# A hybrid recurrent decoder: the decode tails of three branches move into the streamed work, each behind a later gate, and two branches' ways up move further back

## Chip, cores and metric

The program runs on one core of one Trainium2 chip. The metric is the device time of one execution in microseconds; a kernel is timed several times, and its median is what counts. One execution is also profiled, and every row of the trace comes from that one.

## What is computed

Two layers of a decoder on 256 prompt tokens and 8 decode tokens (264 columns in all; the decode tokens bring states of their own). Each layer is a mixer and then a feed-forward network: a dense SwiGLU in the first layer, the best two of eight experts in the second. The mixer, cut to its frame:

```
u = x @ w_in + b_in                     # projections of four branches, and gates
o_a, S1 = _rwkv7(rw, ...)               # RWKV-7: decay, delta rule, per-token scan
o_b, C1, n1, m1 = _mlstm(mqk, mv, ...)  # mLSTM: matrix memory, then head norm
o_c, gS1 = _gla(gq, gk, gv, gg, ...)    # GLA: decaying state, then head rms
o_d, h1 = _rglru(rx, ry, ...)           # RG-LRU: gated linear recurrence
branches = jnp.stack([o_a, o_b, o_c, o_d], axis=2)
up = jnp.einsum('blgc,gcd->blgd', branches, p['w_branch'][l])
gate = jax.nn.sigmoid(gates.reshape(B, L, N_BRANCH, D))
out = jnp.einsum('blgd,blgd->bld', gate, up) @ p['w_out'][l]
```

The prompt part of a branch is done in chunks. The eight decode tokens each take one step from their state, for GLA for instance

```
S = decay * S + k v^T ;  y = q S        # per decode token; S is an output too
```

In this text the **tail** of a branch is this decode step and, for mLSTM and GLA, the norm over heads and the multiplication by the branch's gate that follow it, since the norm runs over all 264 columns at once.

## The kernel before

**Engines.** PE (TensorE) multiplies, DVE (VectorE) and ACT (ScalarE) do the arithmetic between, SP (SyncE) loads weights through a ring of slots, POOL loads states and parameters. Each has its instructions in a fixed order and waits on semaphores that others raise; the names of the steps ("rw.ops", "n1.var") are those of the semaphore groups.

**Branch work.** In each layer the branches come in the order RG-LRU, mLSTM, GLA, RWKV. Their matmuls write `mW`, four banks of PSUM. The work is a chain that changes engines at nearly every step.

**Streamed work.** Beside it stands work that has no tight order. `streamed_work` (L52) lists it: 13 pairs of projections, 16 pairs of gates (four for each branch), and after each gate the way up of the branch one gate earlier (`("up", g, q)`), except RWKV's four, which end the list. A projection or gate pair needs, on ACT, rounding of its weights in two halves (L824) and reading of its two result tiles (L830, L837); on DVE, the difference between weight and rounded weight, in two halves (L1270, "low parts" or "splits"); on PE, 48 matmuls of 264 columns, two thirds with the rounded weight (`XH`, `XL` are the rounded activations and their rest). A way up is four matmuls on PE (fp32), two products with the gate on DVE (L1279) and a sum (L1285). Their results go through `mA`, the other four banks of PSUM, in the order of the list: tile n takes bank n mod 4 and waits until tile n - 4 has been read.

**The order.** Each engine runs the list through its own generator. `filler` (L687) takes a table (`PE_FILL`, `ACT_FILL`, `DVE_FILL`), and `fill("rw.ops")` issues as many streamed items as the table has for that name, ahead of the wait of that name. So the tables decide, engine by engine, how much streamed work lies between two steps of the chain. On DVE `link` (L1214) makes the next instruction wait until the one before has been written.

**Tails.** They are part of the chain. mLSTM's tail begins behind the step ml.cout: a product with the identity spread over 512 columns (`mm(mW, bo, MX)`, ml.dvb), DVE's update of the state, a second such product (ml.dnum), then `head_norm` (L1292 on DVE, L1992 on PE, L845 on ACT): mean, square, variance, root, reciprocal. GLA's (gl.dvb, gl.dy, n2) begins behind gl.y, RWKV's (rw.dsa, rw.dy) behind rw.bonus and ahead of rw.ops, L1593 to L1607 on DVE.

```
PE_FILL:  "rw.g": 19, "rw.dx": 70, "rw.dr": 51, "rw.ops": 49, "rw.again0": 15
DVE_FILL: "rw.bonus": 1, "loads12": 1, "rw.exp": 1, "rw.dsa": 3, "rw.dy": 3, "rw.turn": 4
```

Behind the mixer come a layer norm, the SwiGLU or the experts. They are not touched.

## Time and profile before

| | us |
|---|---|
| runs (three) | 1965.49, 1957.01, 1965.77; median 1965.49 |
| the profiled execution's own time | 1960.32 |
| its span in the profile | 1958.5 |
| PE, DVE, ACT busy in the span | 1805.5, 1383.6, 939.5 |
| mean granted clock of PE | 0.954 |

The span runs from the first to the last instruction of the profiled execution; its own time has 1.8 us more around it. The mixer of layer 0 takes the first 400 us of the span, that of layer 1 from about 620 to 1014 us, the experts the rest. A row of the timeline gives start, duration and instruction, with the idle time of that engine ahead of it and what ended that in square brackets. A granted clock of 1.00 is 2.4 GHz, one of 0.50 is 1.2 GHz; a mean between them is a mix of the two.

### The profile page before, as it was taken

How to read it: one execution, taken by the hardware profiler on the slowest of the kernel's cores; microseconds unless marked ns; L12 is line 12 of the kernel's file. 1: busy time of each engine (PE TensorE's matmuls, PEld its weight loads, DVE VectorE, ACT ScalarE, POOL GpSimd, SP SyncE). 2: the span in 40 equal slices, each digit the busy share in tenths (PEclk: the TensorE clock that was granted, in tenths of full speed). 3: DMA queues.
4: the chain of work that ended last, by engine and by line, in shares of the span. 5: the costliest groups of instructions: out<-in, count | busy, mean ns of one | idle time of the engine just before them, and what ended most of it. 6: DMA issues, size and time to landing. Idle time of an engine off the chain costs nothing.

```text
span 1958.5 us, 26391 instructions
## 1 busy us (share of the span) xinstructions
PE 1805.5 (92%) x10174; PEld 1527.9 (78%) x10174; DVE 1383.6 (71%) x1619; ACT 939.5 (48%) x968; POOL 15.2 (1%) x32
## 2 busy tenths in 40 slices
PE   8799989979998989989986999999899999999896
PEld 7678878879997868868865877777687877777685
DVE  4857864445652758885425988989797979888794
ACT  4323422243332524422214666666576657766673
POOL 1000000000001000000000000000000000000000
PEclk9789999999998979999995999999999999999999
DMA  6233322334552324321223988989798978989770
GB/s 244 94 107 141 123 87 72 124 151 173 186 182 77 130 87 159 127 97 65 109 105 155 343 320 298 346 305 340 272 347 306 340 282 323 346 320 344 278 299 23
DMA packets 59307, 402.81 MB, mean 206 GB/s; under 512 B 8672, under 2 KB 9344, under 8 KB 11312
## 3 DMA queue, kind: packets, MB, share of 16 engines
q1 hardware_dynamic: 54144, 393.73, 54.0%
q0 software_dynamic: 1600, 3.97, 0.6%
q10 hardware_dynamic: 3440, 3.41, 0.5%
q8 instruction: 84, 1.38, 0.3%
q14 instruction: 39, 0.32, 0.0%
HBM read 396.60 MB, written 4.49 MB: 205 GB/s over the span
## 4 chain that ended last, share of the span: by engine, by line
PE 81%; DVE 11%; ACT 4%; issue 3%; DMA 0%; ACTq 0%; DVEq 0%; SPq 0%
PE mA L1906 48%; PE mW L1906 31%; ACT WH L703 2%; DVE slots_rounded L1270 1%; PE mA L1837 1%; DVE SCR L1235 1%; ACT X L994 1%; DVE SCR L1352 0%; DMA slots<-in_w_in_dram 0%; DVE V L1709 0%; DVE SCR L1347 0%; PE mW L1909 0%; DVE BIG L1285 0%; DVE HEL L1172 0%; DVE SCR L1237 0%
## 5 line engine op out<-in xcount | busy, mean ns | idle before, releaser
L1050 DVE TENSOR_TENSOR ring_low<-ring,WH 128x2048 fp32r<-128x2048 f32 x216 | 493.0, 2289 | 92.6 <-ACT WH L703 92.0
L703 ACT ACTIVATE WH<-ring 128x2048 fp32r<-128x2048 f32 x212 | 405.0, 1913 | 79.6 <-PE mW L1906 64.4
L1906 PE MATMUL mA<-XH,slots_rounded 128*128 128x264 f32 x1696 | 378.3, 297 | 10.2 <-DVE slots_rounded L1270 9.2
L1906 PE MATMUL mA<-WH,XEH 128*128 128x512 f32 x704 | 293.9, 418 | 8.2 <-DVE XEL L1140 6.9
L1906 PEld LDWEIGHTS mA<-XH,slots_rounded 128*128 128x128 f32 x1696 | 286.5, 194 | 17.8 <-issue 12.7
L1906 PE MATMUL mA<-WH,XEL 128*128 128x512 f32 x704 | 277.0, 393 | 0.0
L1906 PE MATMUL mA<-ring_low,XEH 128*128 128x512 f32 x608 | 240.2, 395 | 0.0
L1906 PE MATMUL mA<-XL,slots_rounded 128*128 128x264 f32 x672 | 197.2, 293 | 6.5 <-DVE small L1549 5.6
L1906 PEld LDWEIGHTS mA<-WH,XEH 128*128 128x128 f32 x704 | 133.1, 189 | 39.3 <-DVE ring_low L1050 10.6
L1906 PEld LDWEIGHTS mA<-WH,XEL 128*128 128x128 f32 x704 | 132.9, 189 | 31.9
L1906 PEld LDWEIGHTS mA<-XL,slots_rounded 128*128 128x128 f32 x672 | 130.3, 194 | 11.4 <-DVE small L1549 7.3
L1906 PE MATMUL mA<-BIG,slots 128*128 128x264 f32 x512 | 126.3, 398 | 10.8 <-DVE SCR L1630 6.7
L837 ACT ACTIVATE BIG<-mA,half 128x264 f32<-128x264 f32 x64 | 30.5, 480 | 220.1 <-PE mA L1906 220.1
L1906 PE MATMUL mW<-WH,HEH 128*128 128x512 f32 x352 | 114.7, 408 | 19.1 <-DVE HEL L1172 19.1
L1906 PEld LDWEIGHTS mA<-ring_low,XEH 128*128 128x128 f32 x608 | 114.8, 189 | 22.1
L1050 DVE TENSOR_TENSOR more_low<-more_ring,WH 128x2048 fp32r<-128x2048 f32 x48 | 109.9, 2289 | 17.8 <-ACT WH L703 17.6
L1906 PEld LDWEIGHTS mA<-BIG,slots 128*128 128x128 f32 x512 | 97.8, 196 | 29.9 <-DVE SCR L1630 7.2
L1270 DVE TENSOR_TENSOR slots_rounded<-slots,slots_rounded 128x1024 fp32r<-128x1024 f32 x84 | 100.9, 1223 | 17.4 <-ACT slots_rounded L824 15.7
L1906 PE MATMUL mW<-WH,HEL 128*128 128x512 f32 x352 | 112.8, 402 | 0.0
L1012 ACT ACTIVATE FWH<-slots 128x2048 fp32r<-128x2048 f32 x34 | 65.3, 1920 | 76.0 <-PE mA L1906 46.7
L703 ACT ACTIVATE WH<-more_ring 128x2048 fp32r<-128x2048 f32 x48 | 91.9, 1915 | 20.1 <-PE mW L1906 16.6
L755 ACT ACTIVATE HEH<-mA 128x256 fp32r<-128x256 f32 x88 | 33.7, 383 | 137.7 <-PE mA L1837 137.6
(396 smaller groups left out, 3135.7 us busy)
## 6 DMA issues: line engine op xcount, KB each, us to landing
ring<-in_moe_dram SPq DMA_DIRECT2D x216, 1024.0 KB, 4.8
slots<-in_w_in_dram SPq DMA_DIRECT2D x58, 1024.0 KB, 4.8
more_ring<-in_moe_dram SPq DMA_DIRECT2D x48, 1024.0 KB, 4.8
...
```

Source lines behind the costliest of these rows:

```text
L703: nact.activation(WH[:, HI_SLOT[j % PAIR], :], expert_slot(j), ACT.Copy).then_inc(weights_hi, 1)
L755: nact.activation(HEH[:, b, :], mA[:, 2 + b, 0:256], ACT.Copy).then_inc(turned_hi, 1)
L837: nact.activation(GT[:, gate % GR, :], acc("gate", l, gate), ACT.Tanh, scale=0.5, bias=hc("bgate", KT * item[1] + 2 * item[2] + q))\
L994: ins = nact.activation(X[:, j, :], SQ8[:, j, :], ACT.Identity, scale=pc(f"ln{i + 1}g", j), bias=pc(f"ln{i + 1}b", j))
L1012: nact.activation(w.rounded, w.raw, ACT.Copy).then_inc(hi_done, 2)
L1050: v.tensor_tensor(expert_low(j), expert_slot(j), WH[:, HI_SLOT[j % PAIR], :].bitcast(F32), SUB)\
L1235: v.scalar_tensor_tensor(dst[:, i, back:TP], src[:, i, 0:TP - back], pc(w, 4 * i + 3 - back), dst[:, i, back:TP], MUL, ADD)
L1270: v.tensor_tensor(halves_of(w.low, half), halves_of(w.raw, half), halves_of(w.rounded, half).bitcast(F32), SUB).then_inc(lo_done, 1)
L1837: ins = nc.tensor.transpose(mA[:, 2 + b, P * q:P * q + P], HT[:, b, P * q:P * q + P], C("ident"))
L1906: return nc.tensor.matmul(out, w, x, start=start, stop=stop, skip_group_check=True)
```

## The change

Nine pieces of the tails become streamed items of their own. Each stands in the list directly behind a gate (the third of RG-LRU to the third of GLA), and their 22 matmuls write banks of `mA` in turn with the gates' tiles. On DVE, the steps of a tail are items in the stream too, between the two halves of the splits that follow that gate; on ACT the square and the root of the norms, and the stores of the states, come a gate later. The ways up follow their gates at a distance: RG-LRU one gate behind, mLSTM three, GLA two, RWKV at the end. All three tables of fills are new; DVE's may now name any `link` of the chain ("link23": 1). States are loaded earlier by POOL with a semaphore each, stores of decode states count on a semaphore of their own, the scratch tiles lie elsewhere, and three small copies keep operands of the tails alive.

```diff
+TAILS = {(RG, 2): "ml.dvb", (RG, 3): "ml.dnum", (ML, 0): "ml.mean", (ML, 1): "ml.var", (ML, 2): "gl.dvb", (ML, 3): "gl.dy", (GL, 0): "gl.var", (GL, 1): "rw.dsa", (GL, 2): "rw.dy"}
+
+BEHIND = {RG: 1, ML: 3, GL: 2, RW: 4}
 def streamed_work():
     seq = [("u", i) for i in (TMI - 1, TRX, TRY, TMQ, TMK, TMV, TMO, TGQ, TGV, TGG, TR, TK, TV)]
-    late = []
-    for g in (RG, ML, GL, RW):
-        for q in range(4):
-            seq.append(("gate", g, q))
-            late.append(("up", g, q))
-            if len(late) > 1 and late[0][1] != RW:
-                seq.append(late.pop(0))
-    return seq + late
+    gates = [(g, q) for g in (RG, ML, GL, RW) for q in range(4)]
+    ups = list(gates)
+    for n, (g, q) in enumerate(gates):
+        seq.append(("gate", g, q))
+        while ups[0][0] != RW and gates.index(ups[0]) + BEHIND[ups[0][0]] <= n:
+            seq.append(("up",) + ups.pop(0))
+        if (g, q) in TAILS:
+            seq.append(("tail", TAILS[g, q]))
+    return seq + [("up",) + up for up in ups]
...
-PE_FILL = {"loads9": 25, "rg.conv": 95, "ml.qk": 228, "ml.logd0": 16, "ml.kw3": 9, "ml.abs": 7, "ml.h": 44,
+PE_FILL = {"loads9": 25, "rg.conv": 112, "rg1": 473, "ml.gcol": 15, "ml.kw3": 10, "ml.abs": 8, "ml.h": 34,
...
             def link(ins):
                 linked[0] += 1
+                links[0] += 1
+                own = linked[0]
                 ins.then_inc(dve_link, 1)
-                dve.wait_ge(dve_link, linked[0])
+                between[0](f"link{links[0]}")
+                dve.wait_ge(dve_link, own)
...
+                if name == "gl":
+                    dve.wait_ge(decoded_out, 16 * (DECODED * l + 3))
+                    dve.wait_ge(*act_of.at("u.tile", l, 17))
+                    yield from named(v.tensor_tensor(GXX, unit(), over_v(U[:, TGV:TGV + 2, TP:T]), MUL), "gt.dv")
+                    dve.wait_ge(gl_state_in, 16 * (l + 1))
+                    dve.wait_ge(*act_of.at("gl.exp", l))
+                    yield from linked_up(v.tensor_tensor(GS, GS, over_gv(GDX), MUL))
+                if name == "gl.dvb":
+                    dve.wait_ge(*pe_of.at("gt.dvb", l))
...
             def streamed():
-                l, up, n = layer[0], 0, 0
+                l, up, n, behind = layer[0], 0, 0, []
                 for item in STREAM:
+                    if item[0] == "tail":
+                        behind.append(item[1])
+                        continue
                     if item[0] != "up":
                         n += 1
-                        if PLAIN <= n < len(PAIRS):
+                        for name in behind:
+                            yield from tail_of(name)
+                        if n < len(PAIRS) and n >= PLAIN:
...
+                        while behind:
+                            yield from tail_of(behind.pop(0) + " rest")
+                        if TAILS.get(item[1:]) in ("ml.dvb", "gl.dvb", "rw.dsa"):
+                            yield from tail_of(TAILS[item[1:]][0:2])
...
+                    if name == "gl.dvb":
+                        pe.wait_ge(*dve_of.at("gt.dv", l))
+                        out = into(0)
+                        for j in range(2):
+                            ins = mm(out, con[:, CC["gv"] + P * j:CC["gv"] + P * j + P], flat(GXX, j), j == 0, j == 1)
+                            if j:
+                                ins.then_inc(*pe_of.step("gt.dvb"))
+                            yield
...
-                fill("rw.dx")
-                pe.wait_ge(*dve_of.at("rw.dx", l))
-                for j in range(2):
-                    mm(mW[:, j, :], bo, DX[:, j, :, :].rearrange("p b v -> p (b v)"))
-                for j in range(2):
-                    ins = mm(mW[:, 2 + j, :], bo, DY[:, j, :, :].rearrange("p b v -> p (b v)"))
-                ins.then_inc(*pe_of.step("rw.dsa"))
```

What this does to the order is shown at three places. The first is DVE in RG-LRU, from the step behind the decay's exponential (TENSOR_SCALAR 128x530) through the six steps of a series; `slots_rounded` as the result is a low part, `SCR` scratch of the branch. Before:

```order
L1346 TENSOR_SCALAR SCR<-SCR 128x530 [waits lg_act]
L1347 RECIPROCAL SCR<-SCR 128x530 [waits dve_link]
L1348 TENSOR_TENSOR SCR<-SCR 128x530 [waits dve_link]
L1349 TENSOR_TENSOR SCR<-SCR 128x530 [waits dve_link]
L1350 TENSOR_SCALAR SCR<-SCR 128x530 [waits dve_link]
L1352 SCALAR_TENSOR_TENSOR SCR<-SCR 128x530 [waits dve_link] x6
L1353 TENSOR_SCALAR SCR<-SCR 128x530 [waits dve_link]
```

and now:

```order
L1531 RECIPROCAL SCR<-SCR 128x530 [waits dve_link]
L1453 TENSOR_TENSOR slots_rounded<-slots,slots_rounded 128x1024 [waits hi_done]
L1532 TENSOR_TENSOR SCR<-SCR 128x530 [waits dve_link]
L1453 TENSOR_TENSOR slots_rounded<-slots,slots_rounded 128x1024 [waits hi_done]
L1533 TENSOR_TENSOR SCR<-SCR 128x530 [waits dve_link]
L1453 TENSOR_TENSOR slots_rounded<-slots,slots_rounded 128x1024 [waits hi_done]
L1534 TENSOR_SCALAR SCR<-SCR 128x530 [waits dve_link]
L1453 TENSOR_TENSOR slots_rounded<-slots,mg_rounded 128x1024 [waits hi_done]
L1536 SCALAR_TENSOR_TENSOR SCR<-SCR 128x530 [waits dve_link]
L1453 TENSOR_TENSOR slots_rounded<-slots,mg_rounded 128x1024 [waits hi_done]
L1536 SCALAR_TENSOR_TENSOR SCR<-SCR 128x530 [waits dve_link] x3
```

Low parts now stand between the linked steps, each with a wait for ACT's rounding of its half (hi_done); up to the mLSTM's q and k there are 14 halves more than before.

The second place is PE in RWKV. `mW<-SCR,con 128x264` is the bonus product, `128x512` a tail's product, `mA<-XH` and `mA<-XL` streamed matmuls. Before, RWKV's tail stands there, behind 70 streamed items:

```order
L1906 MATMUL mW<-SCR,con 128x264 [waits rw_dve,rw_act]
L1906 MATMUL mW<-SCR,con 128x264
...
L1906 MATMUL mA<-BIG,slots 128x264 [waits mg.up_dve]
L1906 MATMUL mA<-BIG,slots 128x264
L1906 MATMUL mW<-SCR,con 128x512 [waits rw_dve]
L1906 MATMUL mW<-SCR,con 128x512 x3
L1906 MATMUL mA<-XH,slots_rounded 128x264 [waits lo_done,gate.tile_act]
```

Now:

```order
L2021 MATMUL mW<-SCR,con 128x264 [waits rw_dve,rw_act]
L2021 MATMUL mW<-SCR,con 128x264
L2021 MATMUL mA<-XH,slots_rounded 128x264
L2021 MATMUL mA<-SQ_62,con 128x264 [waits n1_dve,n1_act]
L2021 MATMUL mA<-SQ_62,con 128x264 [waits n1_dve]
L2021 MATMUL mA<-XH,slots_rounded 128x264 [waits lo_done,gate.tile_act]
...
L2021 MATMUL mA<-SCR,con 128x512 [waits n1_dve,gt_dve]
L2021 MATMUL mA<-SCR,con 128x512
L2021 MATMUL mA<-XH,slots_rounded 128x264 [waits lo_done,gate.tile_act]
```

RWKV's tail is gone from here. The variance of mLSTM's norm (`SQ_62`) and, 48 streamed matmuls later, the first product of GLA's tail have come in its place, the latter with a wait for DVE (gt_dve).

The third place is DVE in the same stretch, from the reciprocal of RWKV's key norm (128x528) on. Before:

```order
L1577 RECIPROCAL SCR<-SCR 128x528 [waits rw_act]
L1579 SCALAR_TENSOR_TENSOR SCR<-BIG,par,SCR 128x264 [waits dve_link]
L1579 SCALAR_TENSOR_TENSOR SCR<-BIG,par,SCR 128x264
L1279 SCALAR_TENSOR_TENSOR V_59<-BIG,mA 128x264 [waits gate.tile_act,mg.up_pe,dve_link]
L1583 TENSOR_TENSOR BIG<-mW,BIG 128x528 [waits rw_pe]
L1585 SCALAR_TENSOR_TENSOR SCR<-con,SCR 128x256 [waits rw_dve]
L1585 SCALAR_TENSOR_TENSOR SCR<-con,SCR 128x256
L1587 TENSOR_TENSOR SCR<-SCR 128x512 [waits dve_link]
L1589 TENSOR_TENSOR SCR<-SCR 128x16 [waits rw_dve]
L1590 TENSOR_TENSOR SCR<-con,BIG 128x1024
```

and now, from the same reciprocal to gt.dv, the row that PE's product above waits for:

```order
L1706 RECIPROCAL SCR<-SCR 128x528 [waits rw_act]
L1453 TENSOR_TENSOR slots_rounded<-slots,slots_rounded 128x1024 [waits hi_done,n1_dve]
L1453 TENSOR_TENSOR slots_rounded<-slots,slots_rounded 128x1024 [waits hi_done]
...
L1383 RECIPROCAL SQ_62<-SQ_62 128x528 [waits n1_act]
L1712 TENSOR_TENSOR BIG<-mW,BIG 128x528 [waits rw_pe,dve_link]
L1714 SCALAR_TENSOR_TENSOR SCR<-con,SCR 128x256 [waits rw_dve]
...
L1384 TENSOR_TENSOR V_59<-V_59,SQ_62 128x528 [waits tail_link]
L1716 TENSOR_TENSOR SCR<-SCR 128x512 [waits dve_link]
...
L1391 SCALAR_TENSOR_TENSOR BIG<-V_59,par,BIG 128x264 [waits tail_link]
L1393 SCALAR_TENSOR_TENSOR BIG<-V_59,par,BIG 128x264
L1399 TENSOR_TENSOR SCR<-con,BIG 128x1024 [waits u.tile_act,decoded_out,mt_dve]
```

The end of mLSTM's tail (`SQ_62`, `V_59`), with a reciprocal of its own, now lies between RWKV's steps and ahead of gt.dv.

## Rows read from the trace of the kernel before

**Rows 1.** The page: busy time by engine; the chain by engine.

```profile
PE 1805.5 (92%) x10174; PEld 1527.9 (78%) x10174; DVE 1383.6 (71%) x1619; ACT 939.5 (48%) x968; POOL 15.2 (1%) x32
...
PE 81%; DVE 11%; ACT 4%; issue 3%; DMA 0%; ACTq 0%; DVEq 0%; SPq 0%
```

**Rows 2.** Windows A to D: length, busy PE, PEld, DVE, ACT, POOL, clock, DMA, GB/s.

```profile
9.42:83.89 74.47, 63.78 (x391) 59.20 (x391) 55.72 (x111) 35.69 (x53) 0.54 (x1) 0.90 0.49 183
83.89:127.15 43.26, 41.67 (x216) 31.60 (x215) 16.17 (x25) 8.75 (x16) 0.00 (x0) 0.66 0.16 57
127.15:253.26 126.11, 113.93 (x768) 98.56 (x767) 107.81 (x155) 50.05 (x73) 1.07 (x2) 0.97 0.35 125
253.26:361.04 107.78, 105.81 (x820) 94.23 (x821) 54.74 (x82) 27.18 (x42) 0.00 (x0) 0.99 0.25 89
```

**Rows 3.** Timeline of PE in A and B: its idle times.

```profile
56.48 0.56 PE L1906 MATMUL mA<-XH,slots_rounded 128*128 128x264 f32 x1 [4.05 <-DVE slots_rounded L1270]
...
60.01 0.59 PE L1906 MATMUL mA<-XH,slots_rounded 128*128 128x264 f32 x1 [0.56 <-DVE slots_rounded L1270]
...
80.20 0.59 PE L1906 MATMUL mA<-XH,mg_rounded 128*128 128x264 f32 x1 [5.99 <-DVE slots_rounded L1270]
...
87.92 0.39 PE L1906 MATMUL mA<-XL,mg_rounded 128*128 128x264 f32 x1 [1.58 <-DVE SCR L1414]
```

**Rows 4.** Timeline of PE in C: its idle times.

```profile
146.17 1.16 PE L1906 MATMUL mW<-SQ,con 128*128 128x264 f32 x4 [0.84 <-ACT SQ L849]
...
190.89 0.39 PE L1906 MATMUL mA<-XL,slots_rounded 128*128 128x264 f32 x1 [2.80 <-DVE small L1549]
...
226.12 5.12 PE L1906 MATMUL mW<-SCR,con 128*128 128x512 f32 x8 [2.87 <-DVE SCR L1593]
...
247.92 0.55 PE L1909 MATMUL mW<-con,SCR 128*128 128x128 f32 x3 [1.58 <-DVE SCR L1623]
...
253.26 1.25 PE L1906 MATMUL mA<-BIG,slots 128*128 128x264 f32 x2 [3.37 <-DVE SCR L1630]
```

**Rows 5.** The chain of waits in two windows: start, time, engine, line, count.

```profile
80.20 3.89 PE mA L1906 x16
...
147.33 12.75 PE mA L1906 x105
```

**Rows 6.** Timeline of PE: two of a tail's products, and RWKV's ways up.

```profile
175.71 1.94 PE L1906 MATMUL mW<-SCR,con 128*128 128x512 f32 x4
...
361.04 7.36 PE L1906 MATMUL mA<-BIG,slots 128*128 128x264 f32 x32 [0.78 <-issue]
```

**Rows 7.** Timeline of DVE: a split, q and k, a reciprocal, a tail operation.

```profile
55.10 1.23 DVE L1270 TENSOR_TENSOR slots_rounded<-slots,slots_rounded 128x1024 fp32r<-128x1024 f32 x1
56.25 0.62 DVE L1360 TENSOR_SCALAR SCR<-SCR,small 128x264 f32<-128x264 f32 x2
...
81.70 0.43 DVE L1405 TENSOR_SCALAR SCR<-SCR 128x528 f32<-128x528 f32 x1
...
215.22 3.44 DVE L1577 RECIPROCAL SCR<-SCR 128x528 f32<-128x528 f32 x1
...
222.84 1.22 DVE L1590 TENSOR_TENSOR SCR<-con,BIG 128x1024 f32<-128x1024 f32 x1
```

**Rows 8.** Timeline of ACT: rounding of a half; a table load and a root.

```profile
52.84 1.05 ACT L824 ACTIVATE mg_rounded<-slots 128x1024 fp32r<-128x1024 f32 x1
...
212.23 1.28 ACT L948 ACT_TABLE_LOAD   x1 [1.64 <-DVE SCR L1574]
213.53 0.64 ACT L948 ACTIVATE SCR<-SCR 128x528 f32<-128x528 f32 x1
```

**Rows 9.** Windows behind idle times of PE, columns as in rows 2.

```profile
56.00:65.00 9.00, 7.97 (x34) 7.69 (x35) 8.79 (x15) 5.60 (x8) 0.00 (x0) 0.50 0.05 23
190.89:193.40 2.51, 2.51 (x9) 2.16 (x10) 0.00 (x0) 1.46 (x3) 0.53 (x1) 0.61 0.40 126
193.40:196.80 3.40, 3.40 (x19) 3.00 (x18) 2.01 (x5) 2.83 (x3) 0.00 (x0) 0.78 0.91 370
```

**Rows 10.** Timeline of PE in D: one of its idle times.

```profile
293.01 0.39 PE L1906 MATMUL mA<-XL,slots_rounded 128*128 128x264 f32 x1 [0.47 <-ACT SCR L976]
```

476 lines of the change are left out of this document (281 added, 195 removed), and 16 rows, old and new, of tables (DVE_FILL, PE_FILL).

## Prediction

> **What bounds the kernel now.** I read four views. The page first: TensorE is busy 92% of the span and DVE 71%, and the chain that ended last runs 81% on PE [rows 1]. So a change of order can win only what PE idles or runs at the lower clock, and it loses whatever makes PE wait longer. The table of windows comes next [rows 2]. It cuts layer 0's mixer at four points that both programs have: A from the first matmul to the mLSTM turn (9.42 to 83.89), B the mLSTM block up to its last small product (to 127.15), C from there to the point where RWKV's turned tiles are used (to 253.26), D from there to the ways up of RWKV (to 361.04). Layer 1 has the same four and the same edit. Layer 0's PE is idle 10.7, 1.6, 12.2 and 2.0 us in them, 26.5 together, about 53 in two layers: that is all there is to win, with what the clock takes. Behind D nothing is edited.
>
> The timeline of PE says which waits these are. In A: 4.05, 0.56 and 5.99 us, each for DVE's low parts of a weight [rows 3]; PE reaches the streamed tiles before DVE has split them. In C: 0.84 for a square, then 2.80, 2.87, 1.58 and 3.37 for DVE, three of these in the RWKV stretch [rows 4]. So DVE's place in its own queue sets PE's idle time, although DVE idles 29%.
>
> **Prices.** In the chain 105 streamed matmuls take 12.75 us, 0.1214 each, and 16 behind an idle stretch 3.89, 0.243 each [rows 5]: those are the two levels of the clock. A matmul of a way up costs 7.36 / 16 = 0.46 (two records each), a tail's matmul of 512 columns 1.94 / 2 = 0.97 [rows 6]. On DVE a split of half a weight takes 1.23 us, and what follows it starts 1.15 later; a reciprocal of 528 columns takes 3.44, an operation of 1024 columns 1.22 [rows 7].
>
> **The sum, part by part.** Both programs issue the same matmuls; only places move. I count streamed matmuls (S), matmuls of ways up (U) and RWKV tail matmuls (R) between the anchors in the two orders: A +262 S; B -13 S, +4 U; C -201 S, -4 U, -6 R; D -48 S, +6 R. They add to nothing, so what counts is idle time and clock.
>
> A. 262 x 0.1214 = +31.8. PE now has streamed work of its own until then, behind splits that were issued much earlier, so the waits of 10.6 go, and with them the half clock behind them: in 56 to 65 PE passed 34 matmuls in 9 us at a granted 0.50 where 74 would fit, so about 4.2 lost [rows 9], and the 16 matmuls from 80.20 on lost 3.89 - 1.94 = 1.9. PE alone would be at the turn at 83.9 + 31.8 - 10.6 - 6.1 = 99.0. But DVE must do 14 more halves before it delivers the q and k that the turn takes (L1405, done at 82.13 [rows 7]): 14 x 1.15 = 16.1, so 98.2 by pitch alone. I add 2.3 because the decays' exponentials stand behind more rounding on ACT, and 4.5 for pauses in which DVE waits for ACT's rounding, about 1.0 us a half [rows 8], with four stores issued on ACT ahead of the last half. That gives 105.0, a wait of 6.0 and A at +21.1. Bounds: 99.0 if ACT keeps ahead, 107 if two more halves come late; I take 105.0, since the pauses in rows 3 are of that size.
>
> B. The wait of 1.58 [rows 3] gets 15 streamed matmuls ahead of it and goes; -13 S is -1.6, +4 U is +1.9: -1.3. The window's clock of 0.66 [rows 2] belongs to the block's small matmuls; nothing moves among them, so I leave it.
>
> C. -24.4 (S), -1.9 (U), -5.9 (R) = -32.2. Its waits of 12.2 go with the order that made them, and so does the clock that was low behind 2.80 and 2.87. Behind the first it was 0.61 for 2.51 us and 0.78 for 3.40 [rows 9], which lost 1.0 + 0.7 = 1.7; I take as much behind the second, 3.4 in all: 126.1 - 32.2 - 12.2 - 3.4 = 78.3 of work. New waits take their place. The large one stands at the first matmul of GLA's tail. It is in PE's stream 53 matmuls, some 7 us, behind the RWKV bonus product, and it waits for gt.dv. DVE gets to gt.dv only after: the mLSTM variance 0.7, a reciprocal 3.5, two splits 2.4, two products 0.9, the tail's own reciprocal 3.5, the bonus 0.7, the scans 1.3, the tail's 0.7, products 0.7 + 0.3, then 0.5 + 0.9 of the mLSTM gate, and gt.dv itself 1.2: 17.3, and 1.3 of it the wait for a root. 18.6 - 7 = 11.6 us, in which PE has nothing it may issue. A second of 6.5 stands at the turned tiles: DVE has 22 streamed items in its fill there, one more reciprocal [rows 7] and a root with its table load of 1.28 among them [rows 8], and PE's fill of 126 matmuls covers 15 of about 22. Smaller ones: a bank of gate 3.3 that waits for the product of a way up, GLA's scores and state, 4 together; one stretch at half clock behind the 11.6, 2.9. C = 78.3 + 11.6 + 6.5 + 4.0 + 2.9 = 103.3, or -22.8. Bounds of the two waits: 0 to 20 (0 if DVE were ahead by as much as PE is; 20 if it also waits for PE's product of the mLSTM variance).
>
> The table load shows here as 1.28 us and the activation starts 0.02 after it [rows 8], so a root after a change of table costs 1.3 + 0.6. The Trainium skill (ScalarE: Activation LUTs, "What ACT_TABLE_LOAD costs") gives about 1283 ns for the load, which row and page share, but prices a switch at some 2.7 us with the drain; by that the sum would be an estimated 1.4 us a layer higher. The rows show no such drain, so I leave it out.
>
> D. -48 S is -5.8, +6 R is +5.9. The waits were 2.0: two of 0.47 for ACT's triangular powers (one of them [rows 10]), the 0.78 at its end [rows 6] and crumbs. The fills in this stretch shrink from 3 to 11 matmuls each to 0 to 3 at rw.bk0, rw.l0, rw.e0, rw.e1, rw.s0, rw.z1, and the powers' round trip, 0.47 above a fill of 8, is 1.4 above a fill of 2. Six of these at 0.6 to 1.4 make 6.2 in place of 1.7: +4.5. D = +4.6. Bounds +2 and +9.
>
> Per layer 21.1 - 1.3 - 22.8 + 4.6 = +1.6; two layers +3.2. POOL's state loads go out earlier and gate nothing on PE; SP's queue keeps its order, and the way up of mLSTM, now three gates late, frees the shared slot later, but in the new order GLA's weights have more than eighty streamed matmuls, some 10 us, until they are used; I cost that at nothing, and every microsecond that their load comes too late would add itself in C. The small copies (3 x 0.17) lie in DVE's time and are counted in the pauses. On the profiled execution, 1960.3 (span 1958.5), the sum gives 1963.5. That execution lies 5.2 under the median of the three runs and 3.3 over the lowest, so I put the forecast between: 1966.
>
> **Rivals.**
> *Waits do not materialise (faster).* ACT keeps ahead of DVE, A ends at 99.0 (-6.0), and DVE comes to gt.dv that much earlier, which takes 4.6 from the 11.6. For: DVE has 18.8 us without work in A in the windows (74.47 - 55.72), more than the 16.1 added. Against: it was late all the same, three times [rows 3]. 1.6 - 10.6 = -9.0 a layer, -18.0: 1942.3 on the profiled execution, 1945 on the forecast's footing. It decides where PE's wait at the turn is under 1 us.
>
> *The clock falls behind each long wait (slower).* Behind 5.99 of idle PE ran its 16 matmuls at 0.243 [rows 3, 5], and 56 to 65, behind 4.05, was granted 0.50 throughout [rows 9]. The change ends waits spread over A and puts 11.6 and 6.5 close together in C. If each is followed by 9 us at half clock, 2 x 4.2 replace my 2.9, +5.5 a layer, and the six pauses in D bring one more short stretch, 1.7 by those in C; a layer is then +8.8, two +17.6: 1977.9, or 1980 on the forecast's footing. It decides from two stretches of half clock per layer outside the mLSTM block that last over 5 us. For it: the clock was 0.66 in B and 0.90 in A. Against: behind 2.80 in C the clock was back at 0.78 after 2.51 us [rows 9]. The Trainium skill (TensorE: Matmul & The Clock Gate, "HAM oscillation — how this bites in real kernels") says that waits between groups of matmuls throttle the engine anew and that each wait pays; the 4.05 and 5.99 of [rows 3] agree, and in C the loss behind a wait was smaller [rows 9].
>
> *The tails hold up the chain (slower).* DVE's queue is in order, so a tail's step that waits for PE's product stops the branch behind it. If the mLSTM variance is late by the 2.9 that PE's extra streamed work would make it, RWKV's reciprocals and all that follows shift, and again at GLA's: 2 x 2.9 a layer, 1.6 + 5.8 = +7.4, two +14.8: 1975.1, or 1978.
>
> *It does not do what it says:* the tails could stay next to the chain. The order rules that out, the matmuls stand in the shared banks mA; no chance is given to it.
>
> **How the numbers follow.** Forecast 0.41, faster rival 0.31, clock 0.17, tails 0.11. About 0.5%, 9.8 us, is what a measurement of this kernel can tell from no change, so same is 1955.7 to 1975.3. The faster rival lies below that, both slower ones above; some spill of the forecast either way evens out. The likeliest case has 1956 to 1976 for itself, by the bounds of A and D. The range reaches to 1940, past the middle of the faster rival, and to 1982, past the slower ones' figures.
>
> **What would show it.** In the profile after: A near 95 us long with one PE wait of 4 to 7 at the turn and none for a low part; C near 103 with 10 us or more in front of the first 512-column matmul that goes to mA; 5 or more at the turned tiles; D near 112 with several waits of 0.6 to 1.4. I am wrong if C has no wait over 5 us, if A ends under 101, or if stretches at half clock outside B exceed 10 us a layer.

## The result and the profile after

The changed kernel takes 1940.34 us (median of 4 runs, 1939.53 to 1942.24) where the kernel before takes 1961.49 (4 runs beside them). The ratio is 0.9894 with a 95% interval of 0.9863 to 0.9925: faster by about 1%. The forecast was 1966.0, no change; 1940.34 lies just inside the lower end of the range. Four more runs of the same kernel later, with the experiments, gave 1939.18 to 1946.46.

The page of the changed kernel, its busy times and the chain by engine, answers to [rows 1]. PE is busy 11.8 us less with the same matmuls, and DVE 9.3 us less:

```profile
PE 1793.7 (92%) x10174; PEld 1518.3 (78%) x10174; DVE 1374.3 (71%) x1623; ACT 939.9 (48%) x968; POOL 15.2 (1%) x32
...
PE 80%; DVE 11%; issue 4%; ACT 4%; DMA 0%; ACTq 0%; DVEq 0%; SPq 0%
```

The windows A to D of the changed kernel, layer 0 and then layer 1, with the columns of [rows 2]:

```profile
9.38:100.99 91.61, 89.44 (x653) 85.50 (x653) 68.53 (x123) 50.25 (x74) 0.54 (x1) 1.00 0.61 221
100.99:141.70 40.71, 40.71 (x210) 31.12 (x210) 12.06 (x25) 6.91 (x14) 0.00 (x0) 0.66 0.12 45
141.70:240.73 99.03, 80.66 (x547) 69.24 (x546) 84.49 (x135) 40.31 (x58) 1.07 (x2) 0.94 0.27 93
240.73:350.05 109.32, 105.69 (x785) 91.05 (x785) 64.46 (x92) 24.11 (x37) 0.00 (x0) 0.96 0.24 91
618.15:710.45 92.30, 90.38 (x653) 86.03 (x653) 70.74 (x125) 55.71 (x81) 5.81 (x11) 0.97 0.50 176
710.45:745.24 34.79, 34.79 (x210) 26.95 (x210) 12.06 (x25) 6.91 (x14) 0.00 (x0) 0.80 0.14 55
745.24:844.56 99.32, 80.95 (x546) 69.50 (x545) 84.49 (x135) 40.31 (x58) 1.07 (x2) 0.94 0.26 93
844.56:954.77 110.21, 107.49 (x785) 91.86 (x785) 64.47 (x92) 24.11 (x37) 0.00 (x0) 0.95 0.24 91
```

Layer 0's mixer took 351.62 us before [rows 2] and takes 340.67; layer 1's took 346.02 and takes 336.62. That is 20.4 of gain, of which the unedited rest of the program gives back 2.4: the span went from 1958.5 to 1940.5.

The timeline of PE shows the idle times of layer 0 that answer to [rows 3, 4]:

```profile
100.99 0.33 PE L2024 MATMUL mW<-con,BIG 128*128 128x128 f32 x1 [2.10 <-DVE SCR L1589]
...
157.60 1.14 PE L2021 MATMUL mW<-SCR 64*128 64x256 f32 x8 [0.99 <-DVE SCR L1653]
...
204.14 3.71 PE L2021 MATMUL mA<-SCR,con 128*128 128x512 f32 x4 [10.78 <-DVE SCR L1399]
...
240.73 5.65 PE L2021 MATMUL mW<-SCR 64*128 64x256 f32 x16 [5.77 <-DVE SCR L1745]
...
255.25 1.16 PE L2021 MATMUL mW<-BIG,SCR 128*128 128x128 f32 x8 [0.94 <-DVE BIG L1762]
...
275.32 1.16 PE L2021 MATMUL mW<-SQ 128*128 128x128 f32 x8 [0.85 <-DVE SQ L1776]
```

The first stands at the turn (L1589 is q and k), the third at gt.dv (L1399), the fourth at the turned tiles (L1745); the last two are of D. Set against the prediction's own terms, layer 0:

| stretch | length forecast | measured | idle PE forecast | measured |
|---|---|---|---|---|
| A | 95.6 | 91.61 | 6.0 | 2.10 |
| B | 42.0 | 40.71 | 0 | 0 |
| C | 103.3 | 99.03 | 22.1 | 18.34 |
| D | 112.4 | 109.32 | 6.2 | 3.61 |
| sum | 353.3 | 340.67 | 34.3 | 24.05 |

Of the 12.6 us that the forecast was too long here, 10.3 are idle time of PE. With the same terms layer 1 would take 347.7 and took 336.62.

Where the 10.95 us of layer 0 come from: PE's idle time, A to D, went from 10.6, 1.6, 12.2 and 2.0 us to 2.10, 0, 18.34 and 3.61; that is 8.5 won in A, 1.6 in B, 7.8 given back in C and D, 2.3 in all. PE's busy time at a granted clock of 0.50, half of which is lost, read from windows over each such stretch in both traces, went from 11.8 us to none in A, from 29.1 to 27.3 in B, from 6.3 to 3.5 in C, and up from 3.1 to 7.9 in D: 5.8 won in all, 5.9 of it in A. The 2.9 that remain are busy time at full clock, 2.5 of it in D; what made it less was not tried.

### The profile page after: what moved, and what is told of

It reads as the page before. It is cut to its first block, busy times and chain, and to the rows that moved or that the text cites. A ratio compares the mean times of both kernels' runs of the same rounds, so it can differ in the third digit from the quotient of the medians.

```text
span 1940.5 us, 26425 instructions
## 1 busy us (share of the span) xinstructions
PE 1793.7 (92%) x10174; PEld 1518.3 (78%) x10174; DVE 1374.3 (71%) x1623; ACT 939.9 (48%) x968; POOL 15.2 (1%) x32
## 4 chain that ended last, share of the span: by engine, by line
PE 80%; DVE 11%; issue 4%; ACT 4%; DMA 0%; ACTq 0%; DVEq 0%; SPq 0%
PE mA L2021 48%; PE mW L2021 30%; DVE slots_rounded L1453 2%; ACT WH L738 2%; PE mA L1952 1%; DVE SCR L1298 1%; DVE SQ L1383 1%; ACT X L1052 1%; ACT slots_rounded L894 0%; DMA slots<-in_w_in_dram 0%; PE mW L2024 0%; DVE V L1824 0%; DVE ring_low L1110 0%; DVE HEL L1232 0%; DVE SQ L1826 0%
## 5 line engine op out<-in xcount | busy, mean ns | idle before, releaser
L2021 PE MATMUL mA<-XH,slots_rounded 128*128 128x264 f32 x1696 | 367.3, 292 | 0.0
L2021 PEld LDWEIGHTS mA<-XH,slots_rounded 128*128 128x128 f32 x1696 | 280.2, 190 | 6.6 <-issue 3.7
L2021 PE MATMUL mA<-XL,slots_rounded 128*128 128x264 f32 x672 | 193.3, 288 | 0.0
L2021 PEld LDWEIGHTS mA<-WH,XEH 128*128 128x128 f32 x704 | 134.2, 191 | 39.9 <-DVE ring_low L1110 10.6
L2021 PE MATMUL mA<-BIG,slots 128*128 128x264 f32 x512 | 121.1, 387 | 2.5 <-DVE BIG L1472 2.5
```

The source lines that it names most:

```text
L2021: return nc.tensor.matmul(out, w, x, start=start, stop=stop, skip_group_check=True)
```

## The experiments

Two theories were set against each other at first. **Waits:** PE's idle time was sized too large, term by term, and the gain is A's waits. **Clock:** the gain is A's half clock, and idle time by itself is worth little. Behind these stood the question of what sets the 10.78 at gt.dv, the largest wait. All experiments are edits of the changed kernel, except the sixth; the eighth is that kernel itself. Runs 1 to 6, 9 and 10 are one execution each, and the eight of the changed kernel lie between 1939.18 and 1946.46: where times differ by less, the argument goes by PE's idle time, which repeats far more closely (run 8). "Idle" is PE's idle time, added up from its timeline.

### 1. Seven halves late (e1_late_splits)

```diff
-DVE_FILL: "link6": 1, "link7": 1, "link8": 1, "link9": 1, "link10": 1, "link13": 1, "link14": 1, "link18": 1
+DVE_FILL: "link18": 8
```

> Change kernel with seven low-part halves taken out of the links 6 to 14 of RG-LRU and issued together at link 18, so that PE reaches one of them some 6 us too early; nothing else moves. Theory 'clock': the gain of stage A was the waits plus the half clock behind them, so one wait of about 6.5 us comes back at about 52 us, PE runs some 9 us at half clock behind it (about 4 us lost), the wait of 2.10 at the mLSTM turn goes: A ends at 101.0 + 6.5 - 2.1 + 4 = 109.4 in layer 0, about +8 a layer, 1957 in all. Rival 'waits only': no clock loss, A ends at 105.4, +4.4 a layer, 1949. Rival 'DVE sets A': DVE's total work up to q and k is the same, so A ends at 101 as before, 1940.

1953.34 us. A is 97.84 and 98.69 long (+6.2, +6.4). One wait for a low part is back, 4.31 us, of the kind of [rows 3]:

```profile
58.01 0.59 PE L2020 MATMUL mA<-XH,slots_rounded 128*128 128x264 f32 x1 [4.31 <-DVE slots_rounded L1452]
```

The wait at the turn stays 2.10. So 6.2 to 6.4 us were lost by a wait of 4.31 (4.46 in layer 1): the other 2 are clock behind it. Both theories have a part; what the early splits are worth in A is shown directly, and it is the wait and its clock together. That the wait at the turn stays says that DVE delivers q and k 6.2 us later too, though its work is the same ("DVE sets A" fell): in DVE's timeline pauses of 3.10 and 3.44 us for ACT's rounding, at 65.60 and 71.40, have come in the place of 0.47, 0.73 and 0.16.

### 2. gt.dv first (e2_gl_first)

```diff
+if TAILS.get(item[1:]) == "gl.dvb":
+    yield from tail_of("gl")
 while behind:
     yield from tail_of(behind.pop(0) + " rest")
```

> Change kernel in which DVE issues gt.dv and the decay of GLA's state ahead of the end of the mLSTM tail (its reciprocal and the four steps behind it) instead of behind it. Theory 'DVE's queue bounds C': the wait of 10.78 ahead of GLA's first tail product falls to 2 to 4, but the 34 streamed matmuls behind it then end some 7 us earlier and PE waits 5 to 8 for rw.ops, which DVE reaches at the same time as before (about 210 in layer 0); gain 1 to 3 us a layer, 1934 to 1938. Rival 'that one wait is the cost': the 10.78 fall by 8 and nothing takes their place, C gets 8 shorter, 1924. Rival: the mLSTM branch comes later and its way up waits, 1940 to 1944.

1945.11 us, no gain where 1 to 3 us a layer were expected. The timeline of PE, two waits in the place of one:

```profile
193.76 1.98 PE L2023 MATMUL mA<-SCR,con 128*128 128x512 f32 x4 [2.58 <-DVE SCR L1399]
...
207.77 0.90 PE L2026 MATMUL mW<-con,SCR 128*128 128x128 f32 x3 [7.92 <-DVE SCR L1739]
```

2.58 + 7.92 = 10.50 for 10.78, and C idles 18.07 where it idled 18.34. GLA's decode step was not late by itself. What PE waits for is DVE's queue, and a step that was drawn forward in it pushed the next one back by as much.

### 3. The turned tiles earlier (e3_turn18)

```diff
-DVE_FILL: "rw.turn": 22, "rw.bk0": 3
+DVE_FILL: "rw.turn": 18, "rw.bk0": 7
...
-                dve.wait_ge(*dve_of.at("gt.branch", l))
                 for i, dst in enumerate((ATK, BTK, KTK, VTK)):
```

> Change kernel in which DVE copies RWKV's turned tiles ahead of the last four steps of GLA's tail (root's reciprocal and the three behind it) instead of behind them; they are issued at the next wait (rw.bk0: 7 items in place of 3, rw.turn: 18 in place of 22). Theory 'DVE's queue bounds C': the 5.77 ahead of the first RWKV product go, with the half clock behind them, C ends 5.8 earlier; about 3 + 2 us come back in D as waits for GLA-delayed steps (first for the operand of RWKV's tail, then for rw.bk0); net -4 to -5 a layer, 1930 to 1932. Rival 'it only moves': the four steps (5.1 us of DVE) delay rw.bk0 by as much as they delayed the copies, 1940. Rival 'PE bounds C': no change in C either, since PE's fill of 126 ends when it ends.

1941.71 us. The wait of 5.77 is gone, C is 93.14 and 93.74 (-5.9, -5.6). But D is 112.01 and 113.09, with a new first wait, for RWKV's decode step, which now stands behind the tiles in DVE's queue:

```profile
240.49 3.23 PE L2020 MATMUL mA<-SCR,con 128*128 128x512 f32 x4 [3.25 <-DVE SCR L1422]
```

Idle is 21.8 in place of 24.05 in layer 0's mixer: 5.8 gone from C, 3.6 back in D. The time is that of the changed kernel. Whether what is left was lost to the clock or to a single execution is taken up with run 13.

### 4. More cover in D (e4_cover)

```diff
-PE_FILL: "rw.e0": 1, "rw.s0": 2, "rw.z1": 2, "rw.s1": 1, "rw.again1": 1
+PE_FILL: "rw.e0": 3, "rw.e1": 2, "rw.wt0": 2, "rw.s0": 8, "rw.z1": 8, "rw.s1": 8, "rw.again1": 4
...
-DVE_FILL: "rw.e1": 2, "rw.s0": 1, "rw.z1": 1, "rw.s1": 1
+DVE_FILL: "rw.e1": 2, "rw.e2": 2, "rw.z0": 1
```

> Change kernel in which RWKV's steps e0, e1 and wt0 of stage D get the ways up and tail products that stood at z1, s1 and again1, and those steps get 28 streamed matmuls from the end of the list instead. Theory 'PE bounds D': the waits of 0.33, 0.85, 0.85, 0.85 and 0.47 in layer 0 fall to one of 0.85 or so, D is 1.5 to 2.5 shorter per layer, 1936. Rival 'the chain bounds D': what PE does in the waits delays the next step and the waits come back one step later, D the same within 0.5, 1940. Rival 'clock': those waits are too short to move the clock, so nothing beyond their own length can be won; a gain above 3 a layer would speak against it.

1960.56 us, a miss: D is 120.83 and 119.83 and idles 9.94 and 9.01, and its clock is 0.92. With more streamed work in its first half PE comes to GLA's way up before its weights are there:

```profile
275.09 1.25 PE L2021 MATMUL mA<-BIG,slots 128*128 128x264 f32 x2 [4.76 <-DMA slots<-in_w_branch_dram]
```

The same wait stands in layer 1 (4.76 at 893.50). The prediction had asked whether the slot that is freed three gates late costs anything. Here the load is issued at 270.36, as the slot comes free, and lands at 275.05. In the changed kernel it is issued at 273.00, lands at 277.72 and is first used at 278.63: it costs nothing there, as the prediction had it, but with 0.9 us to spare, since the use comes 5.6 us behind the freeing and not "some 10".

### 5. mLSTM's first tail steps early (e5_ml_early)

```diff
-DVE_FILL: "link32": 1, "link33": 2, "link34": 1, "gl.og": 1, "link35": 1
+DVE_FILL: "ml.qk1": 2, "ml.qk2": 2, "ml.qk3": 2
...
+if item[1:] == (RG, 1):
+    yield from tail_of("ml")
-if TAILS.get(item[1:]) in ("ml.dvb", "gl.dvb", "rw.dsa"):
+if TAILS.get(item[1:]) in ("gl.dvb", "rw.dsa"):
```

> Edit: the mLSTM tail's first DVE steps (decay of the state, products with k and v) are issued in the stretch where the vector engine stands idle for about 26 us beside the quadratic mLSTM, right behind the second gate's eviction, and six of the halves that were split there come two behind each of the three qk waits. Same work, same matmuls. Theory (in-order vector queue bounds the stretch behind the mLSTM: every us of tail work that leaves it shortens it): the stretch from the mLSTM's last column to rw.turned goes from 99.0 to about 95.8 us a layer (-3.2), the wait at gt.dv from 10.78 to about 7.6; with both layers about 1934 us. Rival (the matrix engine waits there for the chain of dependent steps, not for queue time): the wait stays 10 to 11 us or turns up again within 1 us in a later wait of that stretch, the stretch stays at 98 to 99, time 1938 to 1942.

1945.55 us: the theory fell. C is 98.86 and 98.87, and the wait is what it was, though DVE was busy 82.42 us in C where it was 84.49:

```profile
201.53 2.92 PE L2023 MATMUL mA<-SCR,con 128*128 128x512 f32 x3 [10.78 <-DVE SCR L1399]
```

So "every microsecond of DVE's queue in C counts" is wrong. The changed kernel's timeline of DVE shows why. The first row is the step on the mLSTM variance, the last gt.dv:

```profile
187.67 0.71 DVE L1380 TENSOR_SCALAR SQ<-mA 128x528 f32<-128x528 f32 x1 [2.97 <-PE mA L2021]
...
191.65 2.29 DVE L1453 TENSOR_TENSOR slots_rounded<-slots,slots_rounded 128x1024 fp32r<-128x1024 f32 x2
...
202.86 1.22 DVE L1399 TENSOR_TENSOR SCR<-con,BIG 128x1024 f32<-128x1024 f32 x1
```

At 187.67 DVE had stood 2.97 us for PE's product of that variance. It stands there as long in run 5:

```profile
185.05 0.71 DVE L1380 TENSOR_SCALAR SQ<-mA 128x528 f32<-128x528 f32 x1 [2.97 <-PE mA L2023]
```

So what left the queue ahead of this point did not bring the point nearer; it became idle time of DVE (7.4 us in C up to here where it was 6.2, and 0.7 more behind gt.dv). From 187.67 to 204.08 DVE of the changed kernel idles 0.14 us, while PE runs out of streamed work at 193.36 (204.14 - 10.78).

### 6. Early work alone (e6_early_only)

The kernel before, with A's fills as the change has them and the tails left in the chain:

```diff
-PE_FILL: "rg.conv": 95, "ml.qk": 228, "ml.logd0": 16, "ml.kw3": 9, "ml.abs": 7, "ml.h": 44,
-    "ml.cout": 16, "ml.dq": 45, "ml.out": 32, "n1.sq": 15, "gl.ops": 114
+PE_FILL: "rg.conv": 112, "rg1": 473, "gl.ops": 36
...
```

(ACT's and DVE's fills of A are those of the changed kernel, and `link` takes fills.)

> Edit: the kernel before, with only the first stretch's streamed work drawn forward as the change has it (the loads, rg.conv and rg1 fills of the matrix engine, the scalar and vector engines' fills to match); the tails stay in the chain. Theory (the gain of the first stretch is real by itself, but what was drawn forward was the cover of the tails, so it pays only with the tails streamed): first stretch 91 to 93 us as in the changed kernel (74.5 before, with 287 more streamed matmuls done), then 20 to 27 us a layer of new waits of the matrix engine from the quadratic mLSTM to the end of its tail; total 1965 to 1985. Rival (drawing work forward is the whole gain, the tails' place is worth nothing): 1935 to 1945 us, idle of the matrix engine in the later stretches as in the kernel before, within 3 us a layer.

1988.71 us, slower than both kernels and over the 1965 to 1985 expected. Its windows A to D of layer 0, columns as above:

```profile
9.61:100.05 90.44, 90.36 (x652) 86.13 (x652) 67.49 (x122) 49.55 (x72) 0.54 (x1) 1.00 0.60 220
100.05:138.37 38.32, 29.98 (x138) 20.85 (x138) 9.88 (x20) 4.37 (x12) 0.00 (x0) 0.59 0.08 28
138.37:269.32 130.95, 104.21 (x600) 84.98 (x600) 103.21 (x152) 40.65 (x59) 1.07 (x2) 0.87 0.24 83
```

A is even a little shorter than in the changed kernel, without a wait at its end. But B and C idle 8.34 + 26.74 us in place of 1.58 + 12.18 before: 21.3 of new waits, in the mLSTM block (the longest 4.97 us), at the products and the norm of its tail (1.87, 3.90, 3.63, 1.54) and at the head of GLA (4.01). The streamed work that A takes was the cover of these. So the early work does not win alone: in the change its gain in A stands only because the tails have become streamed work. The tails as streamed work without the early work were not run.

### 7 and 8. Runs 3 and 5 together, and the changed kernel again (e7_combo, e8_after_again)

> Edit: the early mLSTM tail steps of the fifth run, and the turn of the RWKV tiles four halves earlier with no wait for the gated linear attention's branch, as in the third run. Theory (both shorten the same in-order vector queue, at different places, so they add): stretch behind the mLSTM to rw.turned 99.0 to about 90 us a layer, 3 to 4 us of it given back in the last stretch's waits as in the third run; idle of the matrix engine 24.1 to about 18.6 us a layer; time 1926 to 1934 us. Rival (what one removes is where the other's wait reappears): idle 21 to 24 us a layer, time 1938 to 1943.

> No edit: the changed kernel once more, on the same chip as the seventh run. All theories: 1939 to 1943 us. Beside it the profile is a second look at the quadratic mLSTM's stretch: if its length follows the phase of the granted clock and not the program, it is again one of about 34.8, 37.8 or 40.8 us and differs between the layers or from the first look by about 3 us; if the program sets it, 40.7 and 34.8 again, and all waits of the matrix engine within 0.2 us of the first look either way.

1941.78 us (4 runs, 1936.75 to 1945.54) against 1943.01 for the changed kernel on the same chip. Idle is 20.97 and 21.80 us a layer, against 23.18 and 22.95 in this second profile of the changed kernel, far from the 18.6 expected: C idles 6.3 less (12.03), but D idles 4.1 and 5.1 more. The medians are 1.2 apart, inside the spread of either. D was 116.07 and 112.80 long. So not even the small part of the idle time that went shows in the time; run 13 was made for this.

The second profile also shows B, columns as above:

```profile
101.30:139.05 37.75, 37.75 (x210) 29.30 (x210) 12.06 (x25) 6.92 (x14) 0.00 (x0) 0.73 0.13 49
711.40:749.26 37.86, 37.86 (x210) 29.27 (x210) 12.07 (x25) 6.92 (x14) 0.00 (x0) 0.73 0.14 51
```

B was 40.71 and 34.79 in the first profile, with the same instructions and no idle time, at granted clocks of 0.66 and 0.80; here it is 37.75 and 37.86 at 0.73. Its length follows the clock and not the program, and a layer can differ by 3 us between executions for this alone. The waits are those of the first profile within 0.2 us, but for D's 0.94, which is not there.

### 9. Variance step behind its split (e9_var_after_split)

```diff
-DVE_FILL: "rw.ksqrt": 1, "link44": 2
+DVE_FILL: "rw.ksqrt": 3
...
 for name in behind:
-    yield from tail_of(name)
+    if name != "ml.var":
+        yield from tail_of(name)
...
+if "ml.var" in behind:
+    yield from tail_of("ml.var")
```

> Edit: at the mLSTM's variance the vector engine does its two halves of the weight first and then the step on the variance (so far the step first, then the halves, 2.29 us, behind it). Nothing leaves the queue; two halves change places with one step for which the queue stood 2.97 us. Theory after the fifth run (the wait at gt.dv is set only by what the vector engine does between the last point at which it waited for the matrix engine, the variance at 185.0, and gt.dv at 201.4; what leaves the queue ahead of that point only makes the engine wait longer there): the halves fall into the 2.97 us, the wait at gt.dv goes from 10.78 to about 8.5, and since the RWKV operands come earlier too, the stretch behind the mLSTM shortens by 2.3 us a layer. Rival one (the wait is conserved, as in the second run): gt.dv 8.5, but 2 us more at rw.turn or rw.turned. Rival two (the whole queue from the mLSTM on counts): nothing changes, 10.78 and 99.0.

1952.26 us, a miss to the other side: the wait at gt.dv grew to 13.18. The two halves could not be done in the 2.97 us, since their rounding was not there. From the timeline of DVE:

```profile
189.84 2.36 DVE L1454 TENSOR_TENSOR slots_rounded<-slots,slots_rounded 128x1024 fp32r<-128x1024 f32 x2 [5.18 <-ACT slots_rounded L894]
...
192.12 0.70 DVE L1380 TENSOR_SCALAR SQ<-mA 128x528 f32<-128x528 f32 x1
```

ACT was late because ahead of this rounding (188.69) its queue has the issue of four stores, a square, and a root between two table loads of 1.28 us each (185.06 and 187.02, the root 186.35). By the Trainium skill ("ScalarE: Activation LUTs", "What ACT_TABLE_LOAD costs") a switch costs some 2.7 us with its drain; here too the activation starts 0.01 behind the load's end (185.06 + 1.28, then 186.35), so the rows show 1.3 and no drain. What follows: gt.dv moved by what was put behind the 2.97 us (the 2.4 that the wait grew by are the two halves, 2.36), and a split is only free in a gap for which ACT has its half ready.

### 10. Two halves out of A's end (e10_two_halves_later)

```diff
-DVE_FILL: "link26": 1, "link27": 1, "link28": 1, "ml.silu": 1
+DVE_FILL: "link26": 1, "ml.qk1": 1, "ml.qk2": 1, "ml.silu": 1
```

> Edit: the last two halves that the vector engine splits ahead of the mLSTM's q and k go behind the first two of its waits for the qk products, where it stands idle. Theory (the first stretch now ends at the vector engine, 2.1 us behind the matrix engine, which would be at the turn at 98.9): the wait at the turn goes from 2.1 to 0, the stretch is 89.5 to 90 us in layer 0 (91.7 before) and the wait does not turn up later, since the engine is idle there. Rival (the split that then comes later holds up the streamed matmuls): a new wait for a low part of 1 us or more before the mLSTM block ends. On the clock: if the half clock of the mLSTM block is made by the wait at its head, it goes or shrinks below 7 us; if it belongs to the block's own small products, the block stays at 35 to 41 us and loses 7 to 14 us to the clock as without a wait in the sixth run.

1936.16 us, as the theory has it. The wait at the turn is gone, and none comes in its place; gt.dv and the turned tiles are unmoved:

```profile
98.97 0.27 PE L2024 MATMUL mW<-con,BIG 128*128 128x128 f32 x1
...
197.70 3.78 PE L2021 MATMUL mA<-SCR,con 128*128 128x512 f32 x4 [10.78 <-DVE SCR L1399]
...
234.38 5.65 PE L2021 MATMUL mW<-SCR 64*128 64x256 f32 x16 [5.77 <-DVE SCR L1745]
```

The turn is at 98.97: "PE alone would be at the turn at 99.0", said the prediction. And B, with no wait ahead of it, still runs nearly half of its length at half clock (36.19 us at 0.76) without idle time: a wait at its head is not needed for that. That the block's small products make it is likely and not shown.

### 11. Runs 3, 9 and 10 together (e11_three)

> Edit: the third, the ninth and the tenth run's edits together. If each takes its own wait: idle time of the matrix engine about 24.1 - 2.1 - 2.3 - 2.3 = 17.4 us a layer, and 1927 to 1934 us, faster than the changed kernel by about 0.5%. If the idle time that goes is given back by the clock, as in the seventh run (18.8 and 19.8 us of idle in place of 23.2 and 22.9, yet 1941.8 against 1943.0): 1936 to 1942 us.

1939.48 us (6 runs, 1937.10 to 1941.10): the time of the second case, but it decides nothing between the two, as the idle time did not go. It carries run 9's loss: the wait at gt.dv is 13.20. Idle is 20.9 and 21.7 us a layer, not 17.4. (The 18.8 and 19.8 of the expectation are run 7's C and D alone; with A they are the 20.97 and 21.80 above.)

### 12 and 13. Two halves, timed, and with the turned tiles earlier (e12_two_halves_timed, e13_halves_turn18)

The edits are those of runs 10 and 3; the two kernels differ by run 3's edit alone.

> The tenth run's kernel, timed. Theory (the wait at the turn and the clock behind it are the only thing it changes): 1934 to 1938 us, that is 4 to 8 under the changed kernel's 1940 to 1943. Rival (the one execution of the tenth run drew short phases of the clock): 1938 to 1943 us. Waits of the matrix engine as in the tenth run, within 0.2 us, either way.

> Edit: the tenth run's and the third run's edits together. Idle time of the matrix engine about 17 us a layer, 4 to 5 under the tenth run's, all of it taken from the stretch behind the mLSTM. If idle time is worth its own length: 1926 to 1930 us. If the last stretch gives it back, as in the third and seventh run, by its new wait of 3.25 us and by half clock behind it (6 to 9 us lost there in place of 4 to 6): 1933 to 1938 us, the same as the twelfth run.

1937.70 us (6 runs, 1935.51 to 1940.48; 0.9884 of the kernel before, 0.9861 to 0.9906) and 1935.76 (6 runs, 1934.30 to 1937.62; 0.9875, 0.9853 to 0.9897). Run 12's median lies in its theory's range by 0.3 us, and its waits are those of run 10 within 0.2. C and D of layer 0, of run 12 and then of run 13:

```profile
135.40:234.80 99.40, 80.92 (x547) 69.51 (x546) 84.60 (x135) 40.32 (x58) 1.07 (x2) 0.94 0.26 93
234.80:344.25 109.45, 105.82 (x785) 91.07 (x786) 64.47 (x92) 24.10 (x37) 0.00 (x0) 0.96 0.24 91
```

```profile
134.84:228.21 93.37, 80.66 (x546) 69.31 (x546) 80.93 (x131) 38.76 (x57) 1.07 (x2) 0.95 0.27 99
228.21:343.76 115.55, 109.18 (x786) 93.67 (x785) 67.98 (x96) 25.66 (x39) 0.00 (x0) 0.93 0.23 86
```

C wins 6.0 and D loses 6.1 (layer 1: 5.8 and 5.4). Idle is 18.95 us where it was 21.95, not the 17 expected, since C idles 5.75 less and D 2.75 more (6.37). The other 3.4 of D's loss are the same matmuls at a lower clock: PE's busy time times what the clock lacks is 105.82 x 0.04 = 4.2 and 109.18 x 0.07 = 7.6. In layer 1, 3.8 of the 5.4 is idle time. The windows behind the first wait of D, of run 12 and then of run 13, show the stretch:

```profile
234.80:242.80 8.00, 8.00 (x19) 5.36 (x20) 5.97 (x5) 0.00 (x0) 0.00 (x0) 0.50 0.00 0
242.80:250.80 8.00, 7.06 (x34) 4.32 (x33) 5.40 (x13) 0.00 (x0) 0.00 (x0) 0.99 0.00 0
```

```profile
234.43:240.43 6.00, 5.57 (x12) 2.73 (x12) 4.95 (x6) 0.00 (x0) 0.00 (x0) 0.56 0.00 0
240.43:248.43 8.00, 8.00 (x23) 5.20 (x23) 3.94 (x9) 0.00 (x0) 0.00 (x0) 0.50 0.00 0
```

Behind the wait of 5.77 PE ran about 8 us at half clock, behind that of 3.25 about 13. But this part belongs to the single execution. Behind the same 5.77 the changed kernel ran 18 us at half clock in run 8, and behind the same 3.25 run 3 ran 3.4 us; the windows of run 8 and then of run 3, layer 0:

```profile
238.06:256.12 18.06, 18.06 (x41) 10.76 (x42) 10.04 (x15) 0.00 (x0) 0.00 (x0) 0.50 0.00 0
```

```profile
241.09:244.50 3.41, 3.11 (x6) 1.03 (x4) 3.38 (x5) 0.00 (x0) 0.00 (x0) 0.50 0.00 0
244.50:260.00 15.50, 14.55 (x105) 12.54 (x105) 12.51 (x17) 2.66 (x5) 0.00 (x0) 1.00 0.00 1
```

Taken together, D is 112.0 to 116.1 us long with the earlier turn (runs 3, 7, 11 and 13, eight layers; mean 114.4, idle 6.9) and 109.3 to 113.1 without it (the changed kernel twice and runs 1, 2, 5, 9, 10 and 12, sixteen layers; mean 110.4, idle 3.0). So of the 5.8 us that an earlier turn takes from C, about 4 come back in D, nearly all of it as new waits in the same DVE queue; that the clock takes its part as well is not shown, since its share differs as much between executions as between the edits. Some 1.8 us a layer would be left; the medians of runs 12 and 13 are 1.9 apart, too little to tell from nothing.

All six times of run 13 lie under all eight of the changed kernel, whose median is 1940.7, but they were not taken beside each other. Against the kernel before, timed beside each, run 13 stands at 0.9875, run 12 at 0.9884 and the changed kernel at 0.9894 and 0.9884, with intervals that overlap: that either is faster than the changed kernel is not shown. What is shown is the wait of about 2 us at the turn, which run 10's edit removes in both layers.

## Why the prediction was wrong

The mechanism was right and its sizes were not. The waits forecast for PE stand where the prediction put them, and each is smaller. Two of the prediction's three signs of being wrong came: A ended at 100.99, just under 101, and half clock outside B took 11.4 us of PE's time in layer 0 (3.5 behind the 10.78, 7.9 behind the 5.77), over 10; C kept its waits over 5.

- **A, the step that failed first.** The prediction had DVE deliver q and k at 105.0: 16.1 for fourteen halves, 2.3 for the decays' exponentials and 4.5 for pauses in which DVE waits for ACT's rounding. DVE delivered at 100.93 where it had at 82.13 [rows 7]: 18.8, so 2.7 came of the 6.8 added. The timeline of DVE shows the new pauses, 0.47 + 0.73 + 0.16 + 0.98 = 2.34, three of them here, behind two longer ones:

```profile
44.19 0.44 DVE L1530 TENSOR_SCALAR SCR<-SCR 128x530 f32<-128x530 f32 x1 [3.35 <-ACT SCR L939]
...
53.54 1.22 DVE L1453 TENSOR_TENSOR slots_rounded<-slots,mg_rounded 128x1024 fp32r<-128x1024 f32 x1 [0.47 <-ACT mg_rounded L894]
...
59.36 1.23 DVE L1453 TENSOR_TENSOR slots_rounded<-slots,gt_rounded 128x1024 fp32r<-128x1024 f32 x1 [0.73 <-ACT gt_rounded L894]
...
72.50 0.71 DVE L1554 SCALAR_TENSOR_TENSOR SCR<-SCR 128x528 f32<-128x528 f32 x1 [1.99 <-ACT SCR L950]
...
99.02 1.23 DVE L1453 TENSOR_TENSOR slots_rounded<-slots,slots_rounded 128x1024 fp32r<-128x1024 f32 x1 [0.98 <-ACT slots_rounded L894]
100.16 0.43 DVE L1588 TENSOR_SCALAR SCR<-SCR 128x528 f32<-128x528 f32 x1
100.50 0.43 DVE L1589 TENSOR_SCALAR SCR<-SCR 128x528 f32<-128x528 f32 x1
```

  The first is the wait for the decays' exponentials: it was 2.36 before, so it grew by 1.0 where 2.3 were added. The 1.99, for RG-LRU's root, is new and was not in the sum. Up to q and k DVE idles 4.4 us more than before, and the fourteen halves add 14.5 of busy time, not 16.1. The pauses were sized by PE's waits of [rows 3], which are of another engine and another order. PE's side held: 98.89 measured (100.99 - 2.10), 99.0 forecast, and run 10 shows it bare. A came out 4.0 shorter than forecast in layer 0.
- **B.** -1.3 forecast, -2.6 and -4.1 measured. The difference lies within what the clock does to this block by itself (run 8).
- **C.** 11.6 at gt.dv was 10.78, 6.5 at the turned tiles was 5.77, the two large terms within 0.8 us. "4 together" for smaller ones was 1.79: the bank of gate 3.3 made no wait, and GLA's state and the rest made 0.99, 0.31 and 0.49. The 2.9 of half clock behind the 10.78 was 1.8: PE ran at 0.50 for 3.5 us there.
- **D.** Of six waits of 0.6 to 1.4, 6.2 in all, three came over 0.6 (0.94, 0.85, 0.85), with crumbs 3.61. Layer 1 has 2.68. Neither the clock that D lost (2.4 us more than before) nor the 2.5 us less of busy time at full clock was in the sum; that they cancel in layer 0 is luck.
- **Footing.** The forecast stood 2.5 over its sum of 1963.5, for the median of before. The changed kernel's profiled execution is 1.9 over its median, on the other side.

In sum: 23.6 us too long in two mixers (12.6 and 11.0), 21.7 of it idle time; 2.4 of the rest of the program went the other way; 4.4 were footing: 25.6 of the miss of 25.7. The failing step is the sum of the new waits, above all the 4.5 of pauses in A and the round sums for small waits in C and D, each taken at the upper side.

**The rivals.** "Waits do not materialise", 1945, came nearest in time, and half of its mechanism is shown false: the wait at the turn was 2.10, over its own mark of 1 us, and when run 10 took it away, gt.dv's stayed 10.78 and did not shrink by 4.6. DVE idles 28.7 us in B (40.71 - 12.06), so an earlier end of A does not carry over. "The clock falls behind each long wait" is what C and D show: half clock behind 10.78 and 5.77, and the mark of 10 us a layer outside B is passed; its own mark, two stretches of over 5 us, is met by 7.9 and missed by 3.5. But the kernel before lost more to it, 5.9 us in A [rows 9] and 4.7 in C and D where the changed kernel loses 5.7 in C and D alone, so the sum did not turn slower. The windows of the changed kernel behind the 5.77:

```profile
240.73:243.00 2.27, 2.27 (x6) 1.90 (x8) 2.24 (x2) 0.00 (x0) 0.00 (x0) 0.50 0.00 0
243.00:246.00 3.00, 3.00 (x12) 2.28 (x9) 1.41 (x2) 0.00 (x0) 0.00 (x0) 0.50 0.00 0
246.00:249.00 3.00, 3.00 (x5) 1.17 (x4) 2.55 (x3) 0.00 (x0) 0.00 (x0) 0.57 0.00 0
249.00:252.00 3.00, 3.00 (x15) 2.07 (x14) 1.28 (x3) 0.00 (x0) 0.00 (x0) 1.00 0.00 0
```

The rule of the Trainium skill ("TensorE: Matmul & The Clock Gate", "HAM oscillation — how this bites in real kernels"), that each wait between groups of matmuls pays again, agrees with these rows. Behind D's waits under 1 us there is no half clock: from 255 to 300 us it is 1.00. "The tails hold up the chain" came in part: at the variance, where it was feared, DVE stood 2.97 us for PE, close to its 2.9, but what followed was the forecast wait and no more, as the forecast had counted from the product beside that one on.
